# Multi-head latent attention: q from one tile of rotated columns per four heads and two tiles of plain ones

## What is computed

```python
proj = u @ w_in                                   # c_q 512, c_kv 256, k_r 32
q = (rms_norm(c_q, g_q) @ w_uq).reshape(B, S, 16, 96)
q_n, q_r = q[..., :64], apply_rope(q[..., 64:], cos, sin)
kv = (rms_norm(c_kv, g_kv) @ w_ukv).reshape(B, S, 16, 128)
k_n, v = kv[..., :64], kv[..., 64:]
k_r = apply_rope(k_r, cos, sin)
s = (q_n . k_n + q_r . k_r) * 96 ** -0.5          # causal
o = softmax(s) @ v                                # 16 heads
return o @ w_o
```

## Time and profile before

| | |
|---|---|
| median of 3 runs | 1205.27 us (1205.06 to 1205.79) |
| profiled execution: time, span | 1205.41 us, 1203.6 us |
| busy: TensorE, DVE, ACT, POOL | 99%, 51%, 39%, 23% |
| granted TensorE clock | 0.999 of full |
| from the first copy of a turned block of head 0 to that of head 14 | 79.83 to 200.22 us |

### The profile page before, as it was taken

The page is one execution under the profiler, slowest core; times in us unless marked ns, Lnnn a source line. Parts: engine busy times, 40 slices in busy tenths (PEclk is TensorE's granted clock), DMA queues, the critical chain, the costliest instruction groups (busy, mean ns, idle before and its releaser), DMA issues.

```text
span 1203.6 us, 15691 instructions
## 1 busy us (share of the span) xinstructions
PE 1191.9 (99%) x6066; PEld 1006.7 (84%) x6066; DVE 611.3 (51%) x834; ACT 463.5 (39%) x750; POOL 278.5 (23%) x284
## 2 busy tenths in 40 slices
PE   9999999999999999999999999999999999999998
PEld 8878888788888888888889999988888888888887
DVE  6767787554344334334467555656542443433432
ACT  6568888332123112122343255534321221222233
POOL 2323333332002012011202145534210210210212
PEclk9999999999999999999999999999999999999999
DMA  6111113323323332333223534413233232332221
GB/s 205 38 36 36 29 27 104 102 73 105 106 72 104 105 105 75 102 102 105 72 71 109 145 100 105 104 36 105 71 105 105 93 97 91 105 105 90 85 75 71
DMA packets 117514, 107.42 MB, mean 89 GB/s; under 512 B 21350, under 2 KB 115780, under 8 KB 117452
## 3 DMA queue, kind: packets, MB, share of 16 engines
q1 hardware_dynamic: 117420, 106.56, 28.9%
q10 hardware_dynamic: 32, 0.01, 0.0%
HBM read 104.45 MB, written 2.11 MB: 89 GB/s over the span
## 4 chain that ended last, share of the span: by engine, by line
PE 96%; DVE 1%; ACT 1%; issue 1%; POOL 0%; POOLq 0%; DVEq 0%; ACTq 0%
PE ps L1646 27%; PE ps L1648 26%; PE ps L1647 26%; PE ps L1812 1%; PE ps L1782 1%; PE ps L1783 1%; PE ps L1784 1%; PE ps L1824 1%; PE ps L1799 1%; PE ps L2085 1%; PE ps L1827 1%; PE ps L1800 1%; PE ps L1803 1%; PE ps L2087 1%; PE ps L2086 1%
## 5 line engine op out<-in xcount | busy, mean ns | idle before, releaser
L743 ACT CAST whi<-raw 128x2048 fp32r<-128x2048 f32 (+4 forms) x148 | 182.9, 1265 | 262.0 <-PE ps L1648 254.6
L1158 DVE TENSOR_TENSOR wlo<-raw,whi 128x2048 fp32r<-128x2048 f32 (+3 forms) x90 | 197.6, 2198 | 151.8 <-ACT whi L743 151.8
L1646 PE MATMUL ps<-xl,whi 128*128 128x512 f32 (+1 forms) x624 | 245.3, 393 | 0.1
L1648 PE MATMUL ps<-xh,wlo 128*128 128x512 f32 (+1 forms) x624 | 243.1, 390 | 0.0
L1647 PE MATMUL ps<-xh,whi 128*128 128x512 f32 (+1 forms) x624 | 243.1, 390 | 0.0
L1646 PE MATMUL ps<-ul,whi 128*128 128x512 f32 x576 | 224.9, 390 | 0.3 <-DVE wlo L1158 0.3
L1648 PE MATMUL ps<-uh,wlo 128*128 128x512 f32 x576 | 224.4, 390 | 0.0
L1647 PE MATMUL ps<-uh,whi 128*128 128x512 f32 x576 | 224.3, 389 | 0.0
L653 POOL TENSOR_TENSOR ul<-sq,uh 128x512 fp32r<-128x512 f32 x64 | 83.5, 1307 | 521.3 <-ACT uh L1007 521.3
L1398 DVE TENSOR_TENSOR h<-ps,h 128x512 f32<-128x512 f32 x78 | 53.6, 689 | 181.2 <-PE ps L1648 178.0
L1007 ACT CAST uh<-sq 128x512 fp32r<-128x512 f32 x64 | 39.7, 621 | 266.3 <-DVE sq L1430 266.3
(11 more groups left out here) (272 smaller groups left out, 1682.1 us busy)
## 6 DMA issues: line engine op xcount, KB each, us to landing
raw<-in_mlp_w SPq DMA_DIRECT2D x64, 1024.0 KB, 5.3
raw<-in_mlstm_w_in SPq DMA_DIRECT2D x12, 1024.0 KB, 5.3
raw<-in_mla_w_o SPq DMA_DIRECT2D x4, 1024.0 KB, 5.2
raw<-in_mlstm_w_o SPq DMA_DIRECT2D x4, 1024.0 KB, 5.2
raw<-in_mla_w_uq SPq DMA_DIRECT2D x16, 192.0 KB, 2.5
x_tok<-in_x SPq DMA_DIRECT2D x4, 512.0 KB, 7.1
raw<-in_mla_w_in SPq DMA_DIRECT2D x2, 1024.0 KB, 5.6
mx<-m_rows SPq DMA_DIRECT2D x8, 256.0 KB, 3.7
```

Of the source, the lines that this page charges most:

```text
L743: last = sc.copy(hi, src)
L1158: last = v.tensor_tensor(lo, src, hi.bitcast(F32), ALU.subtract)
L1646: mm(o, ah, bl, start=first, stop=False)
L1648: ins = mm(o, al, bh, start=False, stop=last)
```

## The change

q is no longer made by heads. Four heads' 32 rotated columns, unswapped, make one tile of 128 rows (`rope_product`), and the plain columns of a pair of heads another (`nope_product`): 12 tiles in place of 16. The rotated tile is multiplied once by cos and once by sin (`rope_table`), each result split in high and low (`rope_high`, `rope_low`); k's operand now carries the rotated k and its partner turned by a quarter, so no swapped copy is needed. The scale goes into q's norm gains (`query_gains`). The plain tile is split straight from PSUM (`nope_high`, `nope_low`). The parts lie on other partitions than a head's operand wants, so SP puts the operand together by three SBUF to SBUF transfers a head (`place_q`); scores wait for them (`q_in`). Strips hold other columns (N_PAIR to N_WO: 12 of them, not 16), contiguous, with more and smaller loads.

The products of q are spread anew: the rotated tile of group g + 1 in head 4g, plain tiles in 4g + 1 and in 4g + 2 and 4g + 3; some slots are empty or hold three products. The first strip's output products start in head 13 and go in threes by column half (`out_part_1`); six of the second strip's stand before those that need the last pair's output. POOL's low part of an output strip is made in four pieces.

The gate projection's weights leave the strips: they have tiles of their own, high part in columns 0 to 39 and low part in columns 64 to 103 of one stationary operand, so that two matmuls a piece do for three; ACT copies the rows of the low part's product out and DVE adds them.

```diff
+def split_at(head):
+
+    return N_PAIR + 3 + 3 * (head // 4) + (0, 1, 0, 2)[head % 4]
...
+def nope_strip(p):
+
+    return N_PAIR + p if p < 2 else N_PAIR + 3 * (p // 2 - 1) + 3 + p % 2
+
+
+def rope_strip(g):
+
+    return N_PAIR if g == 0 else N_PAIR + 3 * (g - 1) + 2
+
+
+def k_strip(p):
+
+    return N_PAIR if p == 0 else N_PAIR + 3 * ((p - 1) // 2) + 2 + (p - 1) % 2
...
-        tab = A("tab", [P, S])
-        qtmp = A("qtmp", [P, S])
-        pick = Arena(A.at - 4 * 2048)("pick", [16, TT, P], F32R)
+        rope_raw = A("rope_raw", [P, 2, S])
+        pick = nc.alloc_sbuf_tensor_at("pick", [16, TT, P], F32R, offset=acc_at)
...
-        qh = [xh[:, 6 + e, :] for e in range(2)]
-        ql = [xl[:, 6 + e, :] for e in range(2)]
+        q_in_place = [xh[:, 6:8, :], xl[:, 6:8, :]]
+        qh = [t[:, 0, :] for t in q_in_place]
+        ql = [t[:, 1, :] for t in q_in_place]
+        rope_hl = [t[0][:, 1024:2048].rearrange("p (c s) -> p c s", c=2) for t in (whi, wlo)]
+        nope_hl = ul[:, 6:8, :]
...
+        nope_at = {0: 1, 1: 2, 3: 3, 5: 4, 7: 5, 9: 6, 12: 7}
...
+            def load_rope(g):
+
+                heads = a["mla_w_uq"][0].rearrange("(k p) (h n) -> p k h n", p=P, h=HEADS)
+                dst = prope(raw[rope_strip(g) % 2], g)
+                for k in range(4):
+                    sp.dma_start(dst[:, k, :].rearrange("p (e n) -> p e n", e=4),
+                                 heads[:, k, 4 * g:4 * g + 4, NOPE:QK]).then_inc(raw_full[rope_strip(g) % 2], 16)
...
+            def place_q(head):
+
+                e, i, g = head % 2, head // 2, head // 4
+                r = slice(ROPE * (head % 4), ROPE * (head % 4) + ROPE)
+                n, c = slice(64 * e, 64 * e + 64), 64 - 64 * e
+                if head >= 2:
+                    sp.wait_ge(s_mm, 4 * head - 4)
+                sp.wait_ge(n_lo, i + 1)
+                sp.wait_ge(rope_lo, 2 * g + 2)
+                sp.dma_start(q_in_place[e][n, :, :].bitcast(F32), nope_hl[n, :, :].bitcast(F32)).then_inc(q_in[e], 16)
+                for x in range(2):
+                    rows = slice(c + ROPE * x, c + ROPE * x + ROPE)
+                    sp.dma_start(q_in_place[e][rows, :, :].bitcast(F32), rope_hl[x][r, :, :].bitcast(F32)) \
+                        .then_inc(q_in[e], 16)
+
+            slot_free(N_PAIR)
+            load_keys(0)
+            load_rope(0)
+            load_nope(0)
+            load_z(0)
+            load_x(1)
+            place_q(0)
+            place_q(1)
+            load_y(1)
+            for g in range(1, GROUPS):
+                load_z(g)
+                place_q(4 * g - 2)
+                place_q(4 * g - 1)
+                load_x(g + 1)
+                if g + 1 < GROUPS:
+                    load_y(g + 1)
+                else:
+                    load(N_WO, cols(a["mla_w_o"][0], 0))
+                place_q(4 * g)
+                place_q(4 * g + 1)
+            load(N_WO + 1, cols(a["mla_w_o"][0], 256))
+            place_q(HEADS - 2)
+            place_q(HEADS - 1)
+            for j in range(2, 4):
                 load(N_WO + j, cols(a["mla_w_o"][0], 256 * j))
 
...
+            def rope_high(g):
+
+                for e in range(2) if g else ():
+                    act.wait_ge(q_in[e], 48 * 2 * g)
+                for x in range(2):
+                    act.wait_ge(rope_new, 2 * g + x + 1)
+                    sc.copy(rope_hl[x][:, 0, :], rope_raw[:, x, :]).then_inc(rope_hi, 1)
+
+            def nope_high(p):
+
+                for e in range(2) if p else ():
+                    act.wait_ge(q_in[e], 48 * p)
+                act.wait_ge(n_mm, p + 1)
+                sc.copy(nope_hl[:, 0, :], bank(n_bank(p))).then_inc(n_hi, 1)
...
+                if head % 4 != 2 and head + 3 < HEADS:
+                    n = split_at(head)
+                    split(n, "full" if n >= N_WO else head_strip(n))
+                elif head % 4 == 2 and head + 2 < HEADS:
+                    rope_high(head // 4 + 1)
                 if nxt:
                     exp(head + 1, 0)
+                if head in nope_at:
+                    nope_high(nope_at[head])
...
-                if head + 2 < HEADS:
-                    q_high(head + 2)
...
+            def query_gains():
+
+                own.link(v.tensor_scalar(pcol[:, G_Q:G_KV], pcol[:, G_Q:G_KV], SCALE, None, ALU.mult))
...
+            def rope_table(g, x):
+
+                dve.wait_ge(rope_mm, g + 1)
+                if g:
+                    dve.wait_ge(rope_lo, 2 * g)
+                v.tensor_tensor(rope_raw[:, x, :], bank(B_Q), (cos, sin)[x][:], ALU.mult).then_inc(rope_new, 1)
+
+            def rope_low(g):
+                for x in range(2):
+                    dve.wait_ge(rope_hi, 2 * g + x + 1)
+                    low(rope_hl[x][:, 1, :], rope_raw[:, x, :], rope_hl[x][:, 0, :]).then_inc(rope_lo, 1)
+
+            def nope_low(p):
+                dve.wait_ge(n_hi, p + 1)
+                low(nope_hl[:, 1, :], bank(n_bank(p)), nope_hl[:, 0, :]).then_inc(n_lo, 1)
...
+                turning = head % 4 == 0 and head + 4 < HEADS
+                if head % 4 == 2 and head + 2 < HEADS:
+                    rope_low(head // 4 + 1)
                 if nxt:
                     row_max(head + 1, 0)
-                if head + 2 < HEADS:
-                    q_table(head + 2)
+                if turning:
+                    rope_table(head // 4 + 1, 0)
                 pt_low(head, 2)
+                if head in nope_at:
+                    nope_low(nope_at[head])
                 if nxt:
                     row_max(head + 1, 1)
+                if turning:
+                    rope_table(head // 4 + 1, 1)
                 pt_low(head, 3)
                 if nxt:
                     row_max(head + 1, 2)
                     row_max(head + 1, 3)
-                if head + 2 < HEADS:
-                    q_low(head + 2)
                 if i and not second:
                     o_scaled(i - 1)
 
...
+            def out_strip_low(n):
+
+                pool.wait_ge(whi_ready, n + 1)
+                r, hi, lo = raw[n % 2], whi[n % 2], wlo[n % 2]
+                for q in range(4):
+                    c = slice(512 * q, 512 * q + 512)
+                    last = g.tensor_tensor(lo[:, c], r[:, c], hi[:, c].bitcast(F32), ALU.subtract)
+                last.then_inc(wlo_ready, 1)
...
+                        dve.wait_ge(gate_hi, 1)
+                        for src, hi, lo in gate_parts():
+                            ins = low(lo, src, hi)
+                        ins.then_inc(gate_lo, 1)
...
+            dve.wait_ge(g_moved, 1)
+            g_sum = g_low[0:32 + MH, :]
+            own.link(v.tensor_tensor(g_sum, ps[0:32 + MH, T_GATE % RING, :], g_sum, ALU.add))
...
+            def query_product(b, wh, wl, k):
+
+                mm(bank(b), wh[:, k, :], cql[:, k, :], start=(k == 0), stop=False)
+                mm(bank(b), wh[:, k, :], cqh[:, k, :], start=False, stop=False)
+                return mm(bank(b), wl[:, k, :], cqh[:, k, :], start=False, stop=(k == 3))
...
+                    pe.wait_ge(q_in[e], 48 * (head // 2 + 1))
...
+                g, part = divmod(head, 4)
+                ahead = g + 1 < GROUPS
+                if part == 0 and ahead:
+                    rope_product(g + 1, (0, 1))
+                elif part == 1 and ahead:
+                    nope_product(2 * g + 2, (0, 1))
+                elif part == 3 and g + 2 < GROUPS:
+                    nope_product(2 * g + 3, (1,))
+                elif head == HEADS - 4:
+                    nope_product(PAIRS - 1, (2, 3))
                 turn_p(head, 0)
                 turn_p(head, 1)
                 scores(head + 1, 0)
-                if ahead:
-                    q_half(head + 2, 1)
+                if part == 0 and ahead:
+                    rope_product(g + 1, (2, 3))
+                elif part == 1 and ahead:
+                    nope_product(2 * g + 2, (2, 3))
+                elif part == 2 and g + 2 < GROUPS:
+                    nope_product(2 * g + 3, (0,))
+                elif part == 3 and g + 2 < GROUPS:
+                    nope_product(2 * g + 3, (2, 3))
+                elif part == 3:
+                    nope_product(PAIRS - 1, (0, 1))
                 if head % 2:
                     turn_scales(head // 2)
                 turn_p(head, 2)
                 scores(head + 1, 1)
                 turn_p(head, 3)
+                if head == HEADS - 3:
+                    out_part_1(0, 0, (0,))
                 scores(head + 1, 2)
                 scores(head + 1, 3)
                 if head % 2:
                     spread_scales(head // 2)
-                elif ahead:
+                elif head // 2 + 1 < PAIRS:
                     k_product(head // 2 + 1)
                 weigh(head)
 
@@ -1900,49 +2095,54 @@
                 turn_p(head, 0)
...
+                for k in range(5, KD - 1):
+                    for m in range(2):
+                        out_part_1(0, m, (k,))
```

(32 more changed lines are left out.)

305 lines of the change are left out of this document (165 added, 140 removed).

## The result

The changed kernel takes 1211.47 us (median of 5, 1210.28 to 1211.74), the kernel before 1205.58 beside it. The ratio is 1.0046, 95% interval 1.0036 to 1.0057: slower by 5.9 us. I had forecast 1207.1 with a range up to 1211: the side was right, the size was not.

A forecast was written before the change was run, and what follows sets the result against it. The prediction took a loop of ACT and DVE to bound the attention once TensorE's work fell. Loop +2.8, start +2.6, end -1.9 and gate -1.8 make +1.7 on 1205.4: 1207.1 us, range 1200 to 1211.

The forecast's parts named there:

- The start, +2.6: Before the copy of head 0: the first placing is exposed, so that copy comes 2.6 us later (ends +1.8 and +5.3).
- Placing by transfer: SP's three transfers a head: 0.9 for issues plus 2.4 for the last landing, 3.3 us; hidden in the loop.
- now 4.65: At the start, from scores (0, 0) to the copy of head 0: 4.65 us, where it was 6.0 with 1.35 of waiting.
- The loop, +2.8: Heads 0 to 13, copy of head 0 to that of head 14: ACT and DVE take 123.2 us, before 120.4.
- The prices on the chain: Additions to the ACT and DVE loop: nope_high with nope_low 1.08 us a head, rope_high and rope_low 1.1 a head.
- The 0.8 and 0.4 of heads 12 and 13: First output strip: its split, moved to head 12, delays the exponential 0.8 us; o_scaled may wait 0.4 for POOL's piece.
- The end, -1.9: Heads 14 and 15 with fewer output products, -1.1 us; behind the last weigh the 0.75 wait goes, -0.8.
- The gate, -1.8: Gate projection: 16 products do for 24, -1.86 us; late last low of x +0.1; -1.8 (ends -1.9 and -1.0).
- 1 (TensorE bound, 1191.2): Attention loop: TensorE stays the bound, ACT and DVE having more slack than read; 1191.2 us, chance 0.12.
- the 107: TensorE's work in heads 0 to 13, said to fall from 120.4 to some 107 us.
- 3 (late transfers): Last placing lands only 6 us after first issue, start costs +5.3; decides from 4.0 us on; 1209.8 us, chance 0.14.
- 4 (DVE and POOL): Loop: DVE's rope_low runs longer while POOL works, 3 x 1.05 = 3.2 us; 1210.3 us, chance 0.07.

The follow-up runs named there:

- rotated rows first: Changed kernel with head 0's two transfers of rotated rows issued as soon as each is ready, the plain rows last: 1210.71 us.
- the fillers: Changed kernel plus twelve unread products of 512 columns in each of TensorE's waits before scores (0, 0) and (14, 0): 1209.12 us.
- the doubled low: Changed kernel with nope_low done twice, first into an unread buffer, in heads 0, 1, 3, 5, 7, 9 and 12: 1215.81 us.
- the extras moved: Changed kernel with q's nope_high, nope_low, rope_table and rope_low at other places on ACT and DVE, last nope tile a head earlier: 1204.88 us.
- the best kernel: Changed kernel with the extras moved, POOL later, products ahead, rotated rows first, 10 filler products at the start and 6 before scores (14, 0): 1198.81 us.
- POOL later: On the kernel with the extras moved: POOL's four first-strip pieces wait for k_low of heads 14 and 15, three output products go to head 14: 1201.65 us.
- products spread: On the kernel with the extras moved: three products of q go from head 4g+3, ahead of turn_p 0, to head 4g+2: 1205.39 us.
- products ahead: On the kernel with the extras moved: a group's last nope products all issued ahead of head 4g+3's wait for k_low: 1205.11 us.
- The second combination: Changed kernel with the extras moved, POOL later, products spread, filler products before scores (0, 0) and (14, 0), rotated rows first: 1201.18 us.

## Why the prediction was wrong, by its own steps

1. **The start, +2.6.** This failed most, by 2.8 us. *Placing by transfer*, 3.3 us, was mis-sized: from the end of nope_low (74.00) to the scores it took 4.55. The third issue came 1.2 us behind the first (0.6 apart, where the earlier trace rows gave 0.47 and 0.9), and its landing took another 3.2, not 2.4. The Trainium skill's rule that I weighed (DMA: Bandwidth & Descriptors, Rules for kernel authors), transfers that do not run in parallel, would have made it 3.6 (3.5, the line through the earlier trace rows worked out again): nearer, and still short. The rows agree with it so far that the two transfers of 128 KB landed after 2.3 us ahead of the one of 256 KB and after 3.1 and 3.2 behind it. The run with the rotated rows first gave 1.31 back. nope_low ended 0.2 later than worked out. And the step *now 4.65* from scores to copy took no account of the clock: 6.07, of which the fillers gave back 1.56; the 4.51 that they left is near the 4.65.
2. **The loop, +2.8.** It came out 1.9 longer. The prices on the chain held (heads 1, 2, 5, 6, 9, 10: 0.9 to 1.0 for 1.08 and 1.1; the doubled low: 0.53 to 0.79 for 0.60, where it counted). Heads 4 to 9 came out at 17.30, 18.07 and 17.30 for 17.3, 17.8 and 17.3. For heads 3, 4, 7 and 8 that was luck: they took as long with the extras off the chain. What I left out is TensorE's wait for k_low in odd heads, with the products of q behind it: heads 10 and 11 took 18.07 and not 16.7 (+1.3), and moving six of these products gave back 0.95. Against that, head 0 was priced with an o_second and an o_add that it doesn't have (heads 0 and 1: 17.00 for 18.4, -1.4; from the copy to the first exponential it took 85.85 - 84.62 = 1.23 and not 2.22).
3. **The 0.8 and 0.4 of heads 12 and 13** became 1.4 more than forecast. The 0.4 for POOL's piece was 0.6 in o_scaled alone, and the rest is mostly the clock behind the wait of 3.04 us: 1.34 by the fillers.
4. **The end, -1.9**: -2.06 by the trace; the 0.75 of the earlier trace rows is gone. Not tried alone. **The gate, -1.8**: -1.5 in the trace, -1.7 alone; the stop near the last low of x is 0.3, not 0.1.
5. **The rivals.** 1 (TensorE bound, 1191.2) is out: in the loop it is nearly full in heads 0 and 1, 4 and 5, 8 and 9 alone. Nor was its own work the 107 that I gave it: 110.4 us of the loop are listed as busy, some of them at the lower clock, and in the best kernel, at full clock, still 110.25. 3 (late transfers) had the right place, the start, at 1.25 over my value (4.55, past the 4.0 from which it was to decide), but in the loop nothing waited for a placing. 4 (DVE and POOL) was right as a mechanism and wrong in place: rope_low did not meet POOL, o_scaled did.

## What to carry to other kernels

If a loop is timed by a chain on two engines, price that chain, but also ask for every wait of the third engine what of its work is queued *behind* it: work ahead of a wait was free here (three products moved: nothing), the same work behind it was not (six products: 0.95 in one head, 0.27 in another, where the next wait took the rest). When a saving empties an engine that was always full, allow for its clock behind each long wait (1.3 to 1.6 us at each of the two in the kernel after); a few filler products buy it back, and so may real ones moved ahead of the wait. A transfer that replaces a write by an engine costs its issues one by one, and a large one delays the small ones behind it: let the piece that is ready last be the only one behind it.

## What the hardware showed that I had not expected

The clock doesn't answer to one wait alone. At the start, about 3.1 us without work were followed by a full clock in the kernel with the extras moved (k_low to copy 14.04), by some 3.4 us at half in the kernel after (15.57) and by some 6.8 in the one with the extras moved and POOL later (16.28). It isn't the code: with products spread or ahead the start is the same as with the extras moved alone, and there it took 15.18 and 15.20. And a wait of 1.51 us was followed by half the clock in head 11 of the kernel with the rotated rows first, where TensorE had been busy 6.0 of the 10 us before; in the kernel after the same wait came behind the same 6.0, and the clock stayed up. The times scatter with it: of the kernel with the extras moved, the fastest run (1203.71) had a mean granted clock of 0.997 and the slowest (1207.43) 0.993, and the runs of the three kernels with the extras moved and the long waits left in (the moved extras, products spread, products ahead) spread over 2.8 to 4.3 us, those of the best over 0.7. The second combination had fillers too, but waits of 1.6 us left in heads 3 and 7; its profiled execution had the full clock throughout, and its runs fell into two groups, 1199.4 to 1201.2 and 1203.3 to 1203.6. Why the same wait ends so differently from run to run stays open.
